# Moving the weight tiles by 128 and 256 bytes in SBUF: four padding sizes edited in an fp32r decoder kernel

## The reference, cut to what matters

```python
for layer in range(DEPTH):
    x = x + 0.5 * swiglu(rmsnorm(x, ffn1_norm[layer]), ffn1_w_in[layer], ffn1_w_out[layer])
    ...
def sq_relu_mlp(u, w_up, w_down):
    return jnp.square(jax.nn.relu(u @ w_up)) @ w_down
```

## The kernel before, in words

| tile | before | before, mod 512 |
|---|---|---|
| XG (X is 64 bytes on) | 16512 | 128 (X: 192) |
| H | 24768 | 192 |
| SL0 = WL0 (the others every 4096 bytes) | 33152 | 384 |
| RB = BIG, R03, R45, R67, PG0 to PG11, CP, RST | 61888 and on | 448 |
| ONES, PK | 201184, 202720 | 480 |
| WH0 (the others every 4096 bytes) | 207872 | 0 |

## Time and profile before

### The profile page before, as it was taken

How to read it: one execution, slowest core, us unless ns; L and a number is a source line. 1 busy time by engine, 2 the same in 40 slices (tenths; PEclk the granted TensorE clock), 3 DMA queues, 4 the chain that set the end, 5 groups by cost and what they waited for, 6 DMA issues and landing times. The chain is left out here.

```text
span 2696.6 us, 49224 instructions
## 1 busy us (share of the span) xinstructions
PE 2615.0 (97%) x21088; PEld 2530.1 (94%) x21088; DVE 1816.8 (67%) x2374; ACT 1408.3 (52%) x1935; POOL 0.2 (0%) x4
## 2 busy tenths in 40 slices
PE   8999999999998899999999999989999999999998
PEld 8999999999987889999999999979988999989998
DVE  6668766666667646766756865878564786756774
ACT  6446655454457255544446566454455545446553
POOL 0000000000000000000000000000000000000000
PEclk9999999999999999999999999999999999999999
DMA  6564546555543234555544555235543555544564
GB/s 248 176 194 164 172 144 201 193 194 193 192 139 114 76 120 149 193 195 188 181 156 158 179 196 180 79 100 194 191 161 102 173 193 194 177 167 145 178 194 133
DMA packets 129865, 450.12 MB, mean 167 GB/s; under 512 B 20208, under 2 KB 21104, under 8 KB 129520
## 3 DMA queue, kind: packets, MB, share of 16 engines
q1 hardware_dynamic: 129504, 446.83, 50.2%
q10 hardware_dynamic: 144, 0.14, 0.0%
HBM read 445.48 MB, written 1.44 MB: 166 GB/s over the span
## 5 line engine op out<-in xcount | busy, mean ns | idle before, releaser
L274 PE MATMUL B<-R,WH 128*128 128x256 f32 x10432 | 2027.6, 280 | 20.0 <-DVE R L1226 8.6
L274 PEld LDWEIGHTS B<-R,WH 128*128 128x128 f32 x10432 | 1659.0, 189 | 32.3 <-issue 9.7
L1011 DVE TENSOR_TENSOR WL<-SL,WH 128x1024 fp32r<-128x1024 f32 x835 | 1006.6, 1223 | 669.3 <-ACT WH L2091 667.9
L274 PE MATMUL B<-R,WL 128*128 128x256 f32 x4480 | 1243.9, 278 | 0.0
L2091 ACT ACTIVATE WH<-SL 128x1024 fp32r<-128x1024 f32 x835 | 862.3, 1053 | 463.8 <-PE B L274 448.1
L274 PEld LDWEIGHTS B<-R,WL 128*128 128x128 f32 x4480 | 846.5, 189 | 0.0
L274 PE MATMUL B<-RB,WH 128*128 128x256 f32 x1984 | 548.8, 277 | 0.3 <-DVE WL L1011 0.3
L274 PE MATMUL B<-RB,WL 128*128 128x256 f32 x1728 | 477.9, 277 | 0.0
L274 PEld LDWEIGHTS B<-RB,WH 128*128 128x128 f32 x1984 | 372.7, 188 | 0.6 <-DVE WL L1011 0.5
L274 PEld LDWEIGHTS B<-RB,WL 128*128 128x128 f32 x1728 | 324.6, 188 | 0.0
L274 PE MATMUL B<-WH,R 128*128 128x512 f32 x480 | 158.0, 401 | 0.0
(11 more groups left out here) (293 smaller groups left out, 1566.7 us busy)
## 6 DMA issues: line engine op xcount, KB each, us to landing
SL<-in_w SPq DMA_DIRECT2D x835, 512.0 KB, 3.3
CP<-in_cp SPq DMA_DIRECT2D x5, 768.0 KB, 4.8
PG<-in_mem SPq DMA_DIRECT2D x1, 1024.0 KB, 12.9
PK<-in_pk SPq DMA_DIRECT2D x1, 594.5 KB, 8.9
XG<-in_xT SPq DMA_DIRECT2D x1, 512.0 KB, 7.3
out<-XG SPq DMA_DIRECT2D x1, 512.0 KB, 2.6
SL<-in_w SPq DMA_DIRECT2D x1, 384.0 KB, 3.6
XG<-in_xT SPq DMA_DIRECT2D x1, 256.0 KB, 5.7
```

Source lines behind the costliest of these rows:

```text
L274: return p.matmul(o, left, right, start=first, stop=final, skip_group_check=True)
L1011: v.tensor_tensor(WL[t % NRAW][:, :], SL[t % NRAW][:, :], WH[t % NSPL][:, :].bitcast(F32), ALU.subtract).then_inc(s_lo, 1)
```

## The change

Four sizes are edited. `ROOM0` shrinks by 32 float32 (128 bytes), `ROOM` and `ROOM1` grow by as much, `ROOM2` shrinks by 64 float32 (256 bytes):

```diff
-        sb("ROOM0", 48)
+        sb("ROOM0", 16)
...
-            names.enter_context(nc.sbuf_tensor("ROOM", [128, 16], F32))
+            names.enter_context(nc.sbuf_tensor("ROOM", [128, 48], F32))
...
-        sb("ROOM1", 16)
+        sb("ROOM1", 48)
...
-        sb("ROOM2", 96)
+        sb("ROOM2", 32)
```

## The result

The kernel after takes 2735.0 us in the median of four executions (2723.94 to 2738.24), the kernel before 2697.16 us in the median of four (2696.16 to 2698.34). The ratio is 1.0133, with a 95% interval of 1.0102 to 1.0164. It is slower, and it also scatters: its executions lie 14 us apart, those of before 2 us. The profiled execution of after took 2722.22 us and is the fastest of five, so its profile shows some 24 us of a loss that is 38 us in the median.

A forecast was written before the change was run, and what follows sets the result against it. The prediction took TensorE's matmul pace to bound the kernel. Its terms, 0 (TensorE) + 0 (copy, subtraction) + 0 (landing) on 2698.34 us, gave a forecast of 2698 us, the median, with a range of 2690 to 2707 us.

The forecast's parts named there:

- What bounds the kernel: Whole run: the pace of TensorE's matmuls alone sets the time, one 256-column matmul starting every 0.1133 us.
- TensorE's pace: All matmuls with weights: the new distance to the moving operand costs 0, bounds -8.1 and +8.1 us.
- The plain float32 matmuls that I called as witnesses: Matmuls at other operand distances, 379 to 380 ns each, cited as showing that distance doesn't matter.
- The copy and the subtraction: ScalarE's copy and VectorE's subtraction feeding the weights: equal phases cost 0, between -0.08 and 0.18 us in all.
- The window with 31.9 us free: A 100 us stretch, taken as VectorE's densest, cited as slack that hides a slower subtraction.
- The landing: DMA of raw tiles, 3.3 us from issue: term 0, at most 3.0 us back if a tenth faster.
- The gain of 0.9 us: Raw tiles' landing: aligned rows need 128 beats instead of 132, estimated 3% less on nine landings.
- (a): Every matmul: the weights' new distance from the moving operand slows TensorE; 2706 us for one cycle, 2714 for two; chance 0.09.
- (b): VectorE's subtraction: operands at one phase share something in SBUF and it runs at half rate; 2760 us; chance 0.02.
- (c): TensorE: the 16 extra cycles are a collision partly removed; 2690 us for one cycle, 2569 for all; chance 0.06.
- (d): Raw tiles' landing: alignment removes ScalarE's DMA waits; at most 2695 us, or 2684 as bound; large form's chance 0.03.
- (e): Tile placement: rounding takes up the shift, so nothing moves; 2698 us; within the 0.79 for no change.

The follow-up runs named there:

- e16: Kernel before with the high tiles still 64 bytes above the activations and the low tiles 128 bytes from them, modulo 256: 2771.06 us, ratio 1.0266.
- e2: Kernel before with only the high tiles moved, by 256 bytes: 2698.62 us, ratio 1.0000.
- e1: Kernel before with only the raw and low tiles moved, by 128 bytes: 2728.05 us, ratio 1.0100.
- e7: Kernel before, tiles in place, the third matmul loading the high part again instead of the low one (computes something else): 2731.81 us, ratio 1.0125.
- e8: Kernel after, tiles in place, low slices of the 256-column matmuls read 128 bytes beside their place (wrong columns): 2696.91 us, ratio 0.9994 to before.
- e9: Kernel before with high and low tiles both moved to distance 0 from the activations, modulo 256: 2791.44 us, ratio 1.0349.
- e4: Weight tiles at the phase of the kernel after, activations 128 bytes lower: 2753.87 us, ratio 1.0205 to the kernel before.
- e3: Kernel before with raw and low tiles, activations and high tiles all moved by 256 bytes: 2697.75 us, ratio 0.9998.
- e5: Kernel before with raw and low tiles, activations and high tiles all moved by 64 bytes: 2698.15 us, ratio 1.0003.
- e13: Kernel before with raw and low tiles, activations and high tiles all moved by 32 bytes: 2697.71 us, ratio 0.9997.

## Why the prediction was wrong, step by step

**What bounds the kernel** was right: TensorE's pace. The loss is there, with 427 matmuls for 443 in a slow window of 50 us.

**TensorE's pace** is the step that failed: its term was put at 0, and within it this: "If the distance mattered, the two kinds should differ now. They don't". Durations and medians of high and low weights being equal, 277 and 277 ns, I read as no effect of the distance. But all matmuls of before run in one stream at one pace. In the slow stretches of after, high and low ones are slow alike (281 and 281 ns), so there a difference between places doesn't show as a difference between two kinds of instruction; it shows as the pace of the whole stream, and before has only one layout and one pace to show. The equality was no evidence of harmlessness. Nor is it a law the other way: in e16 the two kinds do differ, with medians of 282 and 280 ns. The sign that I named for this step, medians of 277 and 277 ns, was blind to the loss, since after has 276 and 276; the other one, the count of matmuls at full clock, shows it (427 in 50 us), but not in every window (885 from 100 to 200 us).

A later sentence, "Modulo 256 it is the distance that `WH` has today (64), which speaks for 0", had the right modulus (e2) and the wrong conclusion: +64 is harmless for the high part in company with -64 for the low part, and not for both (e1, e7). The term taken as 0 measured +32.2 us in the profiled execution, where its bounds of one cycle either way were 8.1 us; the mean loss is 4.2 cycles a matmul, and that in a slow stretch 10.7. The plain float32 matmuls that I called as witnesses were a weak test: their 256 columns take 216 ns from start to start, nearly twice the 113 of an fp32r matmul, so that they are another kind of stream.

**The copy and the subtraction** were right: 1048 and 1225 ns again, and TensorE waits 7.9 + 4.2 us for the weight chain where it waited 8.5 + 6.1. (The window with 31.9 us free for VectorE isn't the densest for it: from 1500 to 1600 us of before 21.6 us are free. Nothing in the sum hung on it.) **The landing** was right: 3.3 us again, and waits of 8.8 us, within the 7 to 17 us that this wait has over all runs. The gain of 0.9 us that was estimated for aligned rows is too small to be seen in that; no run shows it or excludes it.

**The rivals.** (a) named the place, the sign and a price of 8 us per cycle, and got 0.09; its 2706 us were too low by the number of cycles. It deserved more, as the one rival whose price per unit was large and whose distance no row showed. (b) was refuted by the earlier trace rows and is refuted again by e7 and e8. (c) has a share of truth that I hadn't given it: 16 of the 32 cycles that e9 has above 256 are taken away by the places of before. That part had been taken before the change. (d) and (e) fall too: the landing is as before, and the time did move, with the low tiles alone (e1) as well.

**The cause, as far as the runs show it.** Shown: the loss follows the addresses that TensorE loads weights from (e7, e8), relative to the block of activations (e4 against after; e3, e5 and e13 against before), modulo 256 (e2 for the high part), and it comes as extra cycles of the matmul stream, 0 to 16 on top of 272. Argued, not shown: that the partner is the moving operand, which TensorE streams while the next weights are loaded, and that the two reads meet in the same part of SBUF. The activations' block holds nothing else that TensorE reads in these stretches, and the pace shows no link with what ScalarE and VectorE do. Open: why (+64, -64) keeps to 272 cycles while its mirror, (+64, +64) and (-64, -64) have a second, slow pace too, what in an interruption picks one, and whether the 16 cycles above the 256 columns, which no layout took away, are the moving operand's own.

The Trainium skill, "SBUF — State Buffer", section "Who interferes with whom", says that TensorE's port for the moving operand and its port for LDWEIGHTS are independent and that TensorE waits for no one. If that holds for every placement, no layout costs anything, and the time would be 2697 us in every row of the table. The measurements differ, by up to 3.5% (e9), and they decide: no run shows another engine behind the loss, but TensorE's pace did depend on the distance between the weights that it loads and the block of its moving operand.

No experiment beats the kernel before: e8, the lowest, has a ratio of 0.9994 (0.9985 to 1.0004), and it computes something else.

## What to carry to other kernels

Where a stream of fp32r matmuls bounds a kernel, treat the places of its stationary and moving tiles modulo 256 bytes as a tuning parameter: here (0, 0) took 3.5% more than (+64, -64), and a move of the low tiles by 128 bytes, of the kind that any other edit may bring, cost 1.0 to 1.3%. Measure the pace as the distance between starts over long stretches, and look for stretches of the same instructions with two paces. Equal median durations of two kinds of matmul in one stream don't show that another layout would cost nothing. Where the times of a kernel come to scatter over 14 us, as after's do against 2 to 6 us in the groups of before, it may be choosing between two steady paces somewhere, and this can be found in one trace by counting instructions per window.

## What the runs showed of the hardware that was not expected

- TensorE's pace on identical fp32r matmuls (128 stationary, 256 moving columns) takes values from 113.3 to 120.0 ns, 272 to 288 cycles at the full granted clock, by the places of its operands in SBUF.
- With both weights at +64 the stream has two steady paces, 113.33 and 117.78 ns, holds either for up to some 1,500 matmuls, and changes at interruptions: all 58 stretches in the trace of after with 36 or more matmuls and no distance of 135 ns or more keep one pace from end to end, 24 the fast one and 34 the slow one. (-64, -64) and (-64, +64) have the fast pace and a slow one too, of 117.8 and 118.9 ns. In the windows at 600, 1600 and 2200 us the kernel after is fast, slow, fast (444, 427 and 443 matmuls), e7 fast, slow, slow, and e1, with the same distances, slow, fast, fast:

```profile
600.00:650.00 50.00, 50.00 (x427) 50.00 (x426) 33.10 (x37) 24.23 (x29) 0.00 (x0) 1.00 0.56 188
1600.00:1650.00 50.00, 50.00 (x444) 50.00 (x443) 27.09 (x24) 39.56 (x80) 0.00 (x0) 1.00 0.57 191
2200.00:2250.00 50.00, 50.00 (x444) 50.00 (x443) 40.35 (x55) 24.82 (x29) 0.00 (x0) 1.00 0.58 191
```
